# A two-block transformer kernel: the last tile of four outputs, their norms and the way into the next layer by token halves, without clock-holding products

## What is computed

```python
def rms_norm(x, g):
    xf = x.astype(jnp.float32)
    y = xf * lax.rsqrt(jnp.mean(xf * xf, axis=-1, keepdims=True) + EPS)
    return (y * g.astype(jnp.float32)).astype(x.dtype)
...
    for i in range(DEPTH):
        ...
        h = rms_norm(x, g[0])
        m = parallel_conv_mla(h, ...) if i % 2 == 0 else conformer_conv(h, ...)
        x = x + rms_norm(m, g[1])
        h = rms_norm(x, g[2])
        x = x + rms_norm(squared_relu_mlp(h, mlp_w1[i], mlp_w2[i]), g[3])
```

## Time and profile before

| | |
|---|---|
| median of 3 runs | 1744.0 us (1743.93 to 1744.01) |
| the profiled execution | 1742.19 us |
| its span, first to last instruction | 1740.4 us |
| mean granted TensorE clock | 0.995 |
| TensorE busy | 1716.7 us, 99% of the span |
| VectorE, ScalarE, GpSimd busy | 1076.9, 775.7, 949.1 us |
| chain that ended last: TensorE's share | 84% |

### The profile page before, as it was taken

One profiled execution on the slowest core, in us unless ns is written; L12 is line 12 of the kernel. 1 busy time (PEld: TensorE's weight loads), 2 busy tenths in 40 slices (PEclk: granted clock), 3 DMA queues, 4 the chain that ended last, 5 costly groups with the idle time before them and its releaser, 6 DMA issues.

```text
span 1740.4 us, 25887 instructions
## 1 busy us (share of the span) xinstructions
PE 1716.7 (99%) x9327; PEld 1481.2 (85%) x9327; DVE 1076.9 (62%) x1693; ACT 775.7 (45%) x1301; POOL 949.1 (55%) x583
## 2 busy tenths in 40 slices
PE   8999999999999999999999999999999999999999
PEld 6887888989898887778898989989888888888887
DVE  6458657766667779956867676767765254444100
ACT  6338645343434666554544344455366332222221
POOL 3457546555556679755655545575445554444442
PEclk9999999999999999999999999999999999999999
DMA  5522121423232222212231323222210232222332
GB/s 186 137 101 62 34 76 61 146 68 127 74 133 71 99 73 85 97 64 83 85 134 61 134 83 111 85 85 73 100 37 27 83 109 96 96 96 96 105 101 72
DMA packets 46103, 158.84 MB, mean 91 GB/s; under 512 B 5744, under 2 KB 6000, under 8 KB 46000
## 3 DMA queue, kind: packets, MB, share of 16 engines
q1 hardware_dynamic: 46000, 157.45, 27.0%
HBM read 153.10 MB, written 2.10 MB: 89 GB/s over the span
## 4 chain that ended last, share of the span: by engine, by line
PE 84%; DVE 6%; POOL 4%; ACT 2%; issue 2%; DMA 0%; SPq 0%; POOLq 0%; DVEq 0%; ACTq 0%
PE PS L2199 24%; PE PS L2200 24%; PE PS L2201 24%; DVE PS L1461 2%; PE PS L2268 2%; PE PS L2304 1%; POOL acc_p L790 1%; PE PS L2299 1%; PE PS L2300 1%; PE PS L2209 1%; POOL wl L778 1%; PE PS L2461 1%; POOL acc_p L818 1%; DVE PS L1453 1%; PE PS L2241 0%
## 5 line engine op out<-in xcount | busy, mean ns | idle before, releaser
L2200 PE MATMUL PS<-XLR,wh 128*128 128x512 f32 x1216 | 473.3, 389 | 0.0
L638 POOL TENSOR_TENSOR wl<-raw,wh 128x1024 fp32r<-128x1024 f32 x96 | 232.9, 2428 | 261.4 <-ACT wh L1432 120.8
L628 POOL TENSOR_TENSOR wl<-raw,wh 128x1024 fp32r<-128x1024 f32 x105 | 252.9, 2415 | 184.2 <-ACT wh L890 184.1
L2199 PE MATMUL PS<-XHR,wh 128*128 128x512 f32 x888 | 347.5, 391 | 1.4 <-POOL wl L778 1.0
L2201 PE MATMUL PS<-XHR,wl 128*128 128x512 f32 x888 | 345.7, 389 | 0.0
L890 ACT ACTIVATE wh<-raw 128x1024 fp32r<-128x1024 f32 x171 | 179.2, 1057 | 289.6 <-PE PS L2201 246.4
L2200 PEld LDWEIGHTS PS<-XLR,wh 128*128 128x128 f32 x1216 | 228.4, 188 | 46.7
L2199 PE MATMUL PS<-TH,wh 128*128 128x256 f32 (+1 forms) x872 | 250.5, 287 | 0.1
L2200 PE MATMUL PS<-TL,wh 128*128 128x256 f32 (+1 forms) x872 | 250.2, 287 | 0.0
L2201 PE MATMUL PS<-TH,wl 128*128 128x256 f32 (+1 forms) x872 | 250.2, 287 | 0.0
L2199 PEld LDWEIGHTS PS<-XHR,wh 128*128 128x128 f32 x888 | 166.7, 188 | 36.5 <-POOL wl L778 1.4
(11 more groups left out here) (373 smaller groups left out, 3402.2 us busy)
## 6 DMA issues: line engine op xcount, KB each, us to landing
raw<-weights SPq DMA_DIRECT2D x287, 512.0 KB, 3.3
X<-x_t SPq DMA_DIRECT2D x8, 256.0 KB, 6.8
out_t<-X SPq DMA_DIRECT2D x8, 256.0 KB, 4.3
KH<-rope_h SPq DMA_DIRECT2D x4, 128.0 KB, 4.8
KL<-rope_l SPq DMA_DIRECT2D x4, 128.0 KB, 5.5
QH<-XHR SPq DMA_DIRECT2D x16, 32.0 KB, 2.0
QL<-XLR SPq DMA_DIRECT2D x16, 32.0 KB, 2.0
pos_i<-positions SPq DMA_DIRECT2D x1, 256.0 KB, 8.6
```

Of the source, the lines that this page charges most:

```text
L628: pool.tensor_tensor(wl[:, WPOS[n]], raw[:, n % RING], wh[:, WPOS[n]].bitcast(F32), ALU.subtract).then_inc(w_lo, 1)
L638: pool.tensor_tensor(wl[:, s], raw[:, j], wh[:, s].bitcast(F32), ALU.subtract).then_inc(w_lo, 1)
L2199: pe.matmul(out, wa, xa, start=start, stop=False)
L2200: pe.matmul(out, wa, xb, start=False, stop=False)
```

## The change

The 512 tokens are cut into LEFT (0 to 255) and RIGHT (256 to 511) from the last output tile up to the first operand tile (k = 0) of the next layer.

- The last tile (`last_tile`; in the MLPs `last_down_tile`) makes all products for LEFT into bank RB, then those for RIGHT into the tile ring's bank. Amid the right ones (at k = 4; in the MLPs at k = 5) stands `stat_left`, the statistics of the left half.
- Square, root, copy, reciprocal, spread, update and the first rounding are each done once per half. `norm_out` holds the left spread and the right statistics; `keep_busy` is gone from it, with its three constants. Elsewhere clock-holding products stay.
- `enter_residual` begins with the left half of k = 0: three products with `wh`; then the right spread; two with `wl`; then the right half of k = 0. From k = 1 on it is as before.
- For m2 and m4 the squares of the last two whole tiles are not added to `ssq` by GpSimd (`DIRECT`); TensorE sums them over the partitions itself, once per half, and the last tile's squares go to `tmp[:, 0]`.
- ScalarE rounds weight block n + 3 of the next layer's start between the halves of k = 0 (`early_operand`), and in the MLPs one weight block is rounded before the last squares, not after.

```diff
+AFTER_NORM = {"m1": "mlp0_up0", "m2": "pw1", "m3": "mlp1_up0", "m4": "w_in_2"}
+DIRECT = {"m2": 2, "m4": 2}
...
-W_SQUARE, W_FACTOR, W_UPDATE, W_MEAN, W_CENTRE, W_VALUES, W_START, W_GATE, W_WARM = 1, 2, 10, 10, 16, (1, 0), 20, 10, 8
+W_MEAN, W_CENTRE, W_VALUES, W_START, W_GATE, W_WARM = 10, 16, (1, 0), 20, 10, 8
...
-                add_output(job, KT - 3)
-                add_output(job, KT - 2)
+                pool.wait_ge(restored, KT // 2 * (layer + 1))
...
+            def early_operand(entry, block):
+                b, kept = R2N[entry] - 1, KT * (R2N[entry] - 1) + 1
+                sc.wait_ge(left_new, b + 1)
+                sc.activation(XH[:, 0, LEFT], new_x(0)[:, LEFT], ACT.Copy, scale=ENTRY_GAIN[entry](0)).then_inc(left_xh, 1)
+                sc.activation(X[:, 0, LEFT], new_x(0)[:, LEFT], ACT.Copy).then_inc(left_x_kept, 1)
+                hi(block)
+                sc.wait_ge(x_new, kept)
+                sc.activation(XH[:, 0, RIGHT], new_right(entry), ACT.Copy, scale=ENTRY_GAIN[entry](0)).then_inc(xh, 1)
+                sc.activation(X[:, 0, RIGHT], new_right(entry), ACT.Copy).then_inc(x_kept, 1)
+                sc.wait_ge(left_x_kept, b + 1)
+                sc.wait_ge(x_kept, kept)
+                sc.activation(ssq[:], X[:, 0], ACT.Square).then_inc(squares, 1)
...
-            def last_square(done, **kw):
-
+            def last_square(job, done, **kw):
+                sc.wait_ge(left_made, OUTPUTS.index(job) + 1)
+                sc.activation(last_squares(job)[:, LEFT], PS[:, RB, LEFT], ACT.Square, **kw).then_inc(left_sq, 1)
+                root_left(job)
                 sc.wait_ge(blocks_done, done)
-                sc.activation(sqb[:, 0], PS[:, RB], ACT.Square, **kw).then_inc(last_sq, 1)
+                sc.activation(last_squares(job)[:, RIGHT], PS[:, right_bank(job), RIGHT], ACT.Square, **kw).then_inc(last_sq, 1)
             def boundary(entry, n):
-                root("m" + entry[1])
-                hi(n + 3)
-                operand(entry)
+                root_right("m" + entry[1])
+                operand(entry, n + 3)
...
+                hi(n + 3)
                 square_m(5)
                 square_m(6)
-                sc.wait_ge(ssq_adds, SSQ_ADDS[JOB[job]] - 1)
-                last_square(n + 1)
-                hi(n + 3)
+                last_square(job, n + 1)
...
-                    v.wait_ge(rb_done, JOB["m" + entry[1]] + 1)
-                    for k in range(KT + 1):
+                    job = "m" + entry[1]
+                    v.wait_ge(left_rb, r)
+                    update_half(LEFT, new_x(0)[:, LEFT], left_new)
+                    factor_right(job)
+                    v.wait_ge(rb_done, JOB[job] + 1)
+                    update_half(RIGHT, new_right(entry), x_new)
+                    for k in range(1, KT + 1):
                         if k < KT:
                             update(k)
-                        if k >= 1:
+                        if k == 1:
+                            v.wait_ge(left_x_kept, r)
+                            split_half(LEFT, new_x(0)[:, LEFT])
+                            v.wait_ge(x_kept, KT * (r - 1) + 1)
+                            split_half(RIGHT, new_right(entry)).then_inc(xl, 1)
+                        else:
                             split(k - 1)
...
+                v.wait_ge(left_sq, n)
+                take(LEFT, RB).then_inc(left_kept, 1)
+                factor_left(job)
                 v.wait_ge(last_sq, n)
-                if bias:
-                    sig(ts(M[:, KT - 1], PS[:, RB], bias(KT - 1), ALU.add), bank_free, T + 1)
-                else:
-                    v.tensor_copy(M[:, KT - 1], PS[:, RB]).then_inc(bank_free, 1 + skip)
-                    v.wait_ge(bank_free, T + 1)
-                factor(job)
+                take(RIGHT, right_bank(job)).then_inc(bank_free, 1 + skip)
+                v.wait_ge(left_kept, n)
+                v.wait_ge(bank_free, T + 1)
...
+            def last_tile(n, job):
+                open_block(n)
+                for half in (LEFT, RIGHT):
+                    if half is RIGHT:
+                        open_tile(TILE0[AFTER_NORM[job]] - 1)
+                    for k in range(KT):
+                        if half is RIGHT and k == 4:
+                            stat_left(job)
+                        ins = products(PS[:, RB if half is LEFT else right_bank(job), half], *weight(n, k), XH[:, k, half], XL[:, k, half], k == 0, k == KT - 1)
+                    if half is LEFT:
+                        ins.then_inc(left_made, 1)
+                ins.then_inc(blocks_done, 1)
...
-                last, ahead = T0 + 3, 0
-                for k in range(KT + 1):
+                last, ahead, job = T0 + 3, 0, "m" + entry[1]
+                pe.wait_ge(left_xh, R2N[entry])
+                for half in (LEFT, RIGHT):
+                    if half is RIGHT:
+                        pe.wait_ge(xh, x0 + 1)
+                    for t in range(3):
+                        if half is LEFT:
+                            open_tile(T0 + t)
+                            pe.wait_ge(w_hi, n0 + t + 1)
+                        pe.matmul(PS[:, (T0 + t) % 4, half], wh[:, WPOS[n0 + t], 0], XH[:, 0, half],
+                                  start=half is LEFT, stop=False)
+                    if half is LEFT:
+                        spread_right(job)
+                        open_block(n0)
+                    else:
+                        open_block(n0 + 2)
+                    for t in range(2):
+                        if half is LEFT and t:
+                            open_block(n0 + 1)
+                        pe.matmul(PS[:, (T0 + t) % 4, half], wl[:, WPOS[n0 + t], 0], XH[:, 0, half], start=False, stop=False)
+                pe.matmul(PS[:, (T0 + 2) % 4], wl[:, WPOS[n0 + 2], 0], XH[:, 0], start=False, stop=False)
+                for k in range(1, KT + 1):
...
+            def stat_part(job, columns):
+                n = JOB[job]
+                parts_of = [ssq[:]] + ([sqb[:, 0], sqb[:, 1]] if job in DIRECT else []) + [last_squares(job)]
+                for i, x in enumerate(parts_of):
+                    for j in columns:
+                        ins = pe.matmul(PS[:, STAT, j:j + 1], x[:, j * P:(j + 1) * P], ones[:, 0:1],
+                                        start=(i, j) == (0, columns[0]), stop=(i, j) == (len(parts_of) - 1, columns[-1]))
+                return ins
+            def stat_left(job):
+                n, b = JOB[job], OUTPUTS.index(job)
+                pe.wait_ge(ssq_adds, SSQ_ADDS[n])
+                pe.wait_ge(sd_done, n)
+                if job in DIRECT:
+                    pe.wait_ge(m_squares, (KT - 1) * (b // 2 + 1))
+                pe.wait_ge(left_sq, b + 1)
+                stat_part(job, (0, 1)).then_inc(left_stat, 1)
...
+            def spread_right(job):
+                pe.wait_ge(rcol_done, JOB[job] + 1)
+                pe.wait_ge(bank_free, TILE0[AFTER_NORM[job]])
+                spread_part(job, (2, 3)).then_inc(rb_done, 1)
             def norm_out(job, next_phase, opened=False):
-                n, T = JOB[job], TILE0[next_phase]
+                T, b = TILE0[next_phase], OUTPUTS.index(job)
                 if not opened:
                     open_tile(T)
-                pe.wait_ge(ssq_adds, SSQ_ADDS[n])
-                pe.wait_ge(sd_done, n)
-                for j in range(4):
-                    pe.matmul(PS[:, STAT, j:j + 1], ssq[:, j * P:(j + 1) * P], ones[:, 0:1], start=j == 0, stop=False)
-                keep_busy(W_SQUARE, PS[:, T % 4])
-                pe.wait_ge(last_sq, OUTPUTS.index(job) + 1)
-                for j in range(4):
-                    ins = pe.matmul(PS[:, STAT, j:j + 1], sqb[:, 0, j * P:(j + 1) * P], ones[:, 0:1],
-                                    start=False, stop=j == 3)
-                ins.then_inc(stat_done, 1)
-                keep_busy(W_FACTOR, PS[:, T % 4])
-                pe.wait_ge(bank_free, T)
-                spread(job)
-                keep_busy(W_UPDATE, PS[:, T % 4])
+                pe.wait_ge(left_rcol, b + 1)
+                pe.wait_ge(left_kept, b + 1)
+                spread_part(job, (0, 1)).then_inc(left_rb, 1)
+                pe.wait_ge(left_sd, b + 1)
+                pe.wait_ge(last_sq, b + 1)
+                stat_part(job, (2, 3)).then_inc(stat_done, 1)
...
+                def last_down_tile(n):
+                    open_block(n)
+                    pe.wait_ge(last_m_lo, layer + 1)
+                    for h, half in enumerate((LEFT, RIGHT)):
+                        if h:
+                            pe.wait_ge(products_read, READS * (QUAD0[down_block(layer, NCHUNK - 1)[0]] + QUADS - 1))
+                        bank = PS[:, right_bank(out_job) if h else RB, half]
+                        pe.matmul(bank, ident_r[:], parts(TH, LAST_M, H11 + h), start=True, stop=False)
+                        pe.matmul(bank, ident_r[:], parts(TL, LAST_M, H11 + h), start=False, stop=False)
```

(11 more changed lines are left out.)

95 lines of the change are left out of this document (63 added, 32 removed).

## The result

| | before | changed |
|---|---|---|
| median, 10 runs each, side by side | 1744.01 us (1742.45 to 1746.12) | 1750.85 us (1748.82 to 1756.73) |
| ratio | | 1.0041, 95% interval 1.0031 to 1.0051 |
| profiled execution | 1742.19 us | 1754.56 us |
| its span, mean granted clock | 1740.4 us, 0.995 | 1752.5 us, 0.986 |

The changed kernel is slower by 6.8 us. The page's first part, against the earlier trace rows: TensorE does 100 matmuls more and is busy for 3.7 us more.

A forecast was written before the change was run, and what follows sets the result against it. TensorE, busy for 99% of the span, was taken as the bound. A longer chain (+3.1 us) and clock falls (+3.8) summed to +6.9 on the 1744.0 median: 1750.9 us, range 1745.5 to 1754.5.

The forecast's parts named there:

- a chain of +3.1: Longer wait chain to k=1 to k=3 at full clock, +3.1 us over all four places.
- a clock of +3.8: Clock falls at all four places without holding products: 0.8 us at m1 and m3, 1.1 at m2 and m4.
- The tile: Last output tile, cut in halves with left statistics inside, ends at 6.55 us (m1) and 7.82 us (m2).
- The half operations: Half-width operations on VectorE and ScalarE, such as square 0.39, update 0.49 and scaled rounding 0.47 us.
- The right transposes behind the left products: In TensorE's queue at m1, right transposes wait behind three left products, starting at 9.66 us and ending at 10.05.
- k=1 at m1: TensorE's second operand tile after m1 starts at 13.22 us against 12.80 before, +0.42.
- +0.8 each: Longer chain at m2 and m4, with 16 statistics passes per half: +0.8 us a place at full clock.
- (a): Rival: the clock holds or its fall hits only waiting time, leaving the chain alone, 1747.1 us; chance 0.16.
- (b): Rival: prolonged low clock stretches at m2 and m4, full 1.5 us elsewhere: +11.5, 1755.5 us; chance 0.14.
- (c): Rival: entry, not k=1, sets the place; right update ends by 9.2 us; faster, 1737 us; chance 0.10.
- (d): Rival: left statistics wait for left squares and stall the tile; only a 0.8 us delay would show it.
- the weight rounding: ScalarE's 1.06 us weight rounding between the halves ends at 10.4, before the right update at 11.04: no cost.

The follow-up runs named there:

- e1: Changed kernel with twelve (m1, m3) or eleven (m2, m4) clock-holding products a place put back: 1748.27 us, ratio 1.0024.
- e3: Changed kernel with the four right transposes moved ahead of the wait for the left rounding and the three left products: 1750.68 us, ratio 1.0038.
- e4: e3 with ScalarE's weight rounding also moved, from between the halves to right behind the right squares: 1749.29 us, ratio 1.0028.
- e6: e1 with only the right statistics' passes over the last squares waiting for those squares, the other passes issued earlier: 1747.58 us, ratio 1.0020.
- e8: e1 with GpSimd again summing all squares at m2 and m4, as before the change: 1751.24 us, ratio 1.0039.
- e9: e4 with early right-statistics passes at m2 and m4 only, and fewer clock-holding products put back than in e1: 1746.72 us, ratio 1.0014.
- e10: e3 with all the clock-holding products put back, the weight rounding staying between the halves: 1745.89 us, ratio 1.0014.
- e5: e4 with the clock-holding products of e1 put back: 1744.45 us, ratio 1.0009.
- e2: Kernel before the change without its thirteen clock-holding products at each of the four places, order unchanged: 1750.64 us, ratio 1.0044.

## Why the prediction was right

**Time and mechanism.** Forecast 1750.9 from a chain of +3.1 and a clock of +3.8; measured 1750.85, and e1 shows both terms: about +4.1 for the chain and 2.6 for the clock. That the sum hits to 0.1 us is luck, since the chain was taken some 1 us too low and the clock some 1 us too high. Place by place the forecast was +1.5, +1.9, +1.7 and +1.9 (m1 to m4); the profiled execution has +1.20, +3.58, +2.08 and +1.99, 2 more in all, and is 3.7 above the median.

**The tile.** Forecast end at 6.55 and 7.82 us (m1, m2), measured 6.64 and 8.01. Halving the products cost the forecast 0.32 us: the first 36 take 4.31 us (240.51 to 244.82), 0.12 each. An estimate from the Trainium skill's fixed 2.5 ns a matmul ("TensorE: Matmul & The Clock Gate", "Wait — 56ns, not 53.3ns?") would have been 24 x 2.5 ns = 0.06; the trace does not agree with it.

**The half operations.** 0.38 (square), 0.42, 0.49, 0.43, 0.47 in the trace, against 0.39, 0.43, 0.49, 0.43, 0.47.

**The right transposes behind the left products.** Forecast start 9.66, measured 9.74, and in the path: e3 shows 0.9 us for it. That step was right, its price I had not drawn from it: undoing it alone brings VectorE's update for k=1 back to 10.18 (e3; 10.21 before), and with it the chain of m1 (32.28 in e4 against 32.26 before).

**k=1 at m1.** Forecast 13.22, measured 13.33, and 13.35 with the clock held. k=2 15.65 in e1 against 15.53. The term was +0.72 for m1 and +0.86 for m3; e1 gives 0.93 and 1.00. Of the 0.2 us too little at m1, 0.13 stood there at k=1, and 0.1 came behind k=3: k=3 is at 17.84 (17.02 before, +0.82), and VectorE's 2.2 us a step still set the next step. I had named k=1 on TensorE as what counts; what fits every held place is VectorE's start of the update for k=1, 0.81 later in the changed kernel and 0.89 in e1.

**m2 and m4.** The term was +0.8 each, against a kernel before that has its own falls there. The changed order without a fall was not profiled there. The nearest without one are e6 (34.73, 34.77, with early passes) and e8's m4 (35.01, with the sums), +0.7 to +1.0; e1, with falls as long as those of the kernel before, has +2.1 and +1.4. All four: 3.4 by e6's m2 and m4, 5.4 in e1's trace, forecast 3.1; e1's median gives +4.1. So this term was the least well sized, and its true size is open between these.

**The clock.** It fell at all four places, near 252, 597, 815 and 1163 us, as forecast. Forecast 3.8; 6.8 less e1's 4.1 leaves 2.7, and the medians of e1 and the changed kernel lie 2.6 apart. In e9 it fell with no gap in TensorE's record, which the Trainium skill's warning of long idle gaps (same page, "Why this matters for your kernels") does not cover. Low stretches were longer than I took as the usual case.

**Rivals.** (a) is out: no place held in the profiled execution, and holding the clock gives 2.6 us back (e1). (b) came at one place of the trace: at m2 the clock was low for 10 us, and the place takes 2.8 us more than in e6, where it holds (37.56 against 34.73); (b) had 2.7 for that. The median is not that of (b), and of the profiled execution's 1754.56 some 3.4 are falls outside the four places. (c) is out: the right update ended at 11.1, not 9.2. (d) is out: no wait ahead of the left statistics in the tile. Of the costs taken as nothing, the weight rounding was indeed hidden (e10 and e5).

**What I didn't ask.** The price of the clock depends on the order: in the old order the same removal costs 6.4 us (e2), where I had expected 2 to 4.

## What to carry to other kernels

A result that is ready early is only worth something where the next result in line comes early too: follow each half to the engine that feeds all later steps (here VectorE's update for k=1), not to the first product, and look at what stands ahead of it in the queue of the engine that passes it on. Products that fill waits to hold the clock are part of the schedule: before a change of order is judged at a bound engine, both versions need a held clock, since falls of 3 to 10 us hide differences of 1 us a place. The time of single executions and their mean granted clock read together help to tell whether two medians differ by the order or by the clock: e8 lies 3.0 us above e1 by the median and 0.6 below it among runs at 0.998.

## What the runs showed of the hardware

- Low stretches come also where nothing was changed: 10.2 to 16.6 us in the changed kernel's trace (2.2 us of its time), none there in the trace of the kernel before.
- A fall needs no idle time in the record: in e9 it came within a row of one-column passes and lasted 6.4 us with TensorE busy for 6.40 of it.
- One-column passes slow down with the clock too: eight of them last 1.03 us at full clock (e6) and 1.56 where the clock fell within them (e9).
- A fall costs what lies under it: one of 3 to 4 us cost 0.8 us on dense products at e3's m1, and nothing on the waits at e3's m3.
- GpSimd's sum of two 128 x 512 tiles takes 1.35 us (e8); two of them ahead of the left statistics stall the tile by 1.05 us.
